# Router weights in four column groups, two transposes moved, and the first modulation vectors folded by VectorE

## The reference, cut to what matters

```python
# inside first_block
h = rms_norm(x, norm_mix); z = h @ w_in                      # 2048 columns: pool 512, q, k, v 512 each
y_attn = neighbourhood_attention(q, k, v, q_norm, k_norm, rpb) # 8 heads, a bias from rpb for each pair
x = x + concat(y_pool, y_attn) @ w_out
aff = softmax(rms_norm(x, norm_ffn) @ w_router)              # w_router is 1024 x 16
gates, idx = top_k(aff.T, 64)                                # per expert; then 16 gated experts
x = x + experts(...)
e = rms_norm(p @ w_ple_proj, norm_ple_post)                  # p is 512 x 256
# second_block, first layer
shift, scale, gate = split(silu(c) @ a_ada_w_2 + a_ada_b_2, 3)   # 1024 x 3072: three vectors of 1024
```

## Time and profile before

| what | value |
|---|---|
| median of 3 runs | 2246.3 us (2242.13 to 2247.63) |
| the profiled execution | 2247.05 us, its span 2245.3 us |
| PE busy | 2067.2 us (92%) |
| DVE busy | 906.8 us (40%) |
| ACT busy | 566.2 us (25%) |
| POOL busy | 147.7 us (7%), all of it in the first tenth of the span |
| mean granted clock of TensorE | 0.95 |

### The profile page before, as it was taken

One profiled execution on the slowest core, in us unless ns is written; L12 is line 12 of the kernel. 1 busy time (PEld: TensorE's weight loads), 2 busy tenths in 40 slices (PEclk: granted clock), 3 DMA queues, 4 the chain that ended last, 5 costly groups with the idle time before them and its releaser, 6 DMA issues.

```text
span 2245.3 us, 24651 instructions
## 1 busy us (share of the span) xinstructions
PE 2067.2 (92%) x9349; PEld 1243.1 (55%) x9349; DVE 906.8 (40%) x1457; ACT 566.2 (25%) x973; POOL 147.7 (7%) x86
## 2 busy tenths in 40 slices
PE   6989979999999999999999789999999998989798
PEld 5756763332222222222222277888887786867687
DVE  4754451111111111111111255465455727696963
ACT  4333241111101100011110244432233323553510
POOL 6568000000000000000000000000000000000000
PEclk9965879999999999999999899999999998999899
DMA  8831249999999999999999834553342212011010
GB/s 280 145 114 60 101 169 378 422 422 422 422 422 422 422 423 422 422 422 422 422 422 422 327 113 150 181 180 134 107 159 75 75 40 90 21 57 57 20 38 38
DMA packets 134346, 529.81 MB, mean 236 GB/s; under 512 B 10374, under 2 KB 58308, under 8 KB 85124
## 3 DMA queue, kind: packets, MB, share of 16 engines
q1 hardware_dynamic: 131988, 523.69, 59.4%
q0 software_dynamic: 1712, 3.06, 1.2%
q10 hardware_dynamic: 576, 2.10, 0.4%
HBM read 526.56 MB, written 2.23 MB: 236 GB/s over the span
## 4 chain that ended last, share of the span: by engine, by line
PE 56%; DMA 32%; DVE 7%; SPq 2%; ACT 2%; issue 2%; ACTq 0%; DVEq 0%
DMA w_expert<-in_w_up 15%; DMA w_expert<-in_w_gate 15%; PE bank L784 6%; PE bank L785 6%; PE bank L786 6%; PE bank L972 6%; PE bank L804 5%; PE bank L806 5%; PE bank L805 5%; PE bank L864 2%; SPq L617 2%; PE bank L878 1%; PE bank L816 1%; PE bank L982 1%; DMA raw<-in_w_ple_gate 1%
## 5 line engine op out<-in xcount | busy, mean ns | idle before, releaser
L972 PE MATMUL bank<-w_expert,chosen 128*64 128x512 f32 x2048 | 483.4, 602 | 61.9 <-DMA w_expert<-in_w_up 45.7
L972 PEld LDWEIGHTS bank<-w_expert,chosen 128*64 128x64 f32 x2048 | 130.5, 136 | 395.0 <-issue 233.2
L784 PE MATMUL bank<-act_hi,w_hi 128*128 128x512 f32 x656 | 269.8, 411 | 4.0 <-DVE act_lo L1489 2.0
L1443 DVE TENSOR_TENSOR w_lo<-raw,w_hi 128x2048 fp32r<-128x2048 f32 x75 | 181.9, 2426 | 204.5 <-ACT w_hi L1174 204.5
L786 PE MATMUL bank<-act_hi,w_lo 128*128 128x512 f32 x656 | 256.0, 390 | 0.0
L785 PE MATMUL bank<-act_lo,w_hi 128*128 128x512 f32 x656 | 255.9, 390 | 0.0
L1676 DVE TENSOR_TENSOR x_res<-x_res,bank 128x512 f32<-128x512 f32 x136 | 87.3, 684 | 412.0 <-PE bank L991 412.0
L982 PE MATMUL bank<-w_expert,hidden_t 128*64 128x512 f32 x1024 | 229.9, 596 | 5.8 <-ACT hidden_t L1318 4.6
L1174 ACT CAST w_hi<-raw 128x2048 fp32r<-128x2048 f32 x75 | 142.7, 1902 | 178.1 <-PE bank L806 173.7
L1698 DVE TENSOR_TENSOR hidden_rows<-gate_silu,bank 128x512 f32<-128x512 f32 x32 | 20.5, 683 | 363.7 <-PE bank L972 363.7
L1505 DVE RECIPROCAL full<-full 128x512 f32<-128x512 f32 x38 | 127.3, 3350 | 67.9 <-ACT full L1222 67.9
(11 more groups left out here) (235 smaller groups left out, 2549.7 us busy)
## 6 DMA issues: line engine op xcount, KB each, us to landing
w_expert<-in_w_gate SPq DMA_DIRECT2D x128, 1024.0 KB, 24.9
w_expert<-in_w_up SPq DMA_DIRECT2D x128, 1024.0 KB, 26.2
w_expert<-in_w_down SPq DMA_DIRECT2D x128, 1024.0 KB, 26.2
raw<-in_a_w_in SPq DMA_DIRECT2D x24, 1024.0 KB, 6.1
raw<-in_b_w_in SPq DMA_DIRECT2D x16, 1024.0 KB, 5.3
raw<-in_a_ada_w SPq DMA_DIRECT2D x12, 1024.0 KB, 8.1
raw<-in_b_ada_w SPq DMA_DIRECT2D x12, 1024.0 KB, 6.1
raw<-in_w_in SPq DMA_DIRECT2D x8, 1024.0 KB, 6.7
```

What stands on the lines that cost most here:

```text
L784: mm(b[:, :], hi[:, cols], ah[:, kc, :], start=(kc == 0), stop=False)
L972: last = mm(PS[b0 + n][HALF[x], :], XE[:, k % 4, HALF[k // 4]], WE[place][:, r], start=(k == 0), stop=(k == KD - 1), skip_group_check=True)
L1443: tt(WLO[w % 2][:, :], RAW[slot(n_of["W"][w])][:, :], WHI[w % 2][:, :].bitcast(F32), ALU.subtract).then_inc(lo_ready, 1)
```

## The change

The modulation vectors 0 to 2 are folded by DVE as the later ones are: A slabs 0 to 3 by `split_upto` between the slabs of `w_in`, A slabs 4 to 11 one each at attention items 2, 5, ..., 23. `ada_block` is gone from POOL, so the bias DMAs follow directly on the write-out of `rpb`. The router weights lie padded to 32 columns as stationary operand, one of four groups of 32 columns of the array for chunks kc and kc + 4, with 512 moving columns; ACT copies to four buffers; the four partial sums are added and turned by a second product with a folded identity. The transposes of p and their split stand between the halves of `W_OUT`, with p loaded first of its group. The two memsets stand before the router's result.

```diff
-        FOLD0 = 3
         def fold_done(i):
-            return 2 * (i - 4 * FOLD0 + 1)
+            return 2 * (i + 1)
...
# SP
+            sp.dma_start(PTOK[:, :, :], a["p"][0, 0].rearrange("(t p) d -> p t d", p=P)).then_inc(s_p, 16)
             sp.dma_start(GROW[:, :], bc(a["norm_ffn"], 0, D)).then_inc(s_grow, 16)
             sp.dma_start(CL[:, :], c_late).then_inc(s_late, 16)
-            sp.dma_start(WR[:, :, :], a["w_router"][0].rearrange("(k p) e -> p k e", p=P)).then_inc(s_wr, 16)
-            sp.dma_start(PTOK[:, :, :], a["p"][0, 0].rearrange("(t p) d -> p t d", p=P)).then_inc(s_p, 16)
+            sp.wait_ge(s_wz, 1)
+            sp.dma_start(WR[:, :, 0:NE], a["w_router"][0].rearrange("(k p) e -> p k e", p=P)).then_inc(s_wr, 16)
...
# POOL
-            pool.wait_ge(s_csil, 1)
-            ada_block(0, ACC1)
-
             for c in range(16):
                 pool.dma_start(BIAS[c * ROWS:(c + 1) * ROWS, :, :],
...
-            ada_block(1, ACC1)
-            ada_block(2, ACC1)
...
# PE, behind tm_unit(W_OUT[h], ...)
+                if h == 0:
+                    pe.wait_ge(s_p, 16)
+                    for c in range(2):
+                        b = begin(("pt", c))
+                        for t in range(NT):
+                            last = nc.tensor.transpose(b[:, t * P:(t + 1) * P], PTOK[:, t, c * P:(c + 1) * P], ident)
+                        last.then_inc(filled, 1)
...
             for kc in range(KD):
                 pe.wait_ge(freed["act"], fills[("norm", 1, kc)][2])
-                for t in range(NT):
-                    last = mm(lg[:, t * NE:(t + 1) * NE], FULL[kc % 2][:, t * P:(t + 1) * P], WR[:, kc, :],
-                              start=(kc == 0 and t == 0), stop=(kc == KD - 1), skip_group_check=True)
...
+                part = slice(kc % 4 * 32, (kc % 4 + 1) * 32)
+                last = mm(lg[part, :], WR[:, kc, :], XT4[kc % 4], start=(kc < 4), stop=(kc >= 4), skip_group_check=True)
+                if kc < 4:
+                    last.then_inc(r_used, 1)
+            last.then_inc(filled, 1)
+            pe.wait_ge(freed["act"], fills[("logits",)][2])
+            b = begin(("logits_t",))
+            for t in range(NT):
+                last = mm(b[:, t * NE:(t + 1) * NE], LGT[:, t * P:(t + 1) * P], FOLD[:, :], start=True, stop=True)
+            last.then_inc(filled, 1)
...
# ACT
-                if kc >= 2:
-                    act.wait_ge(r_used, kc - 1)
-                nc.scalar.copy(FULL[kc % 2][:, :], b[:, :]).then_inc(freed["act"], 1)
-            act.wait_ge(freed["dve"], fills[("logits",)][2])
+                if kc == 0:
+                    act.wait_ge(f_lo, f[0])
+                if kc >= 4:
+                    act.wait_ge(r_used, kc - 3)
+                nc.scalar.copy(XT4[kc % 4], b[:, :]).then_inc(freed["act"], 1)
+            nc.scalar.copy(LGT, take(("logits",))[:, :]).then_inc(freed["act"], 1)
+            act.wait_ge(freed["dve"], fills[("logits_t",)][2])
...
# DVE: fold() also for the first twelve slabs, and in the attention
+                    if j % 3 == 2 and len(folded) < 12:
+                        fold(len(folded))
                     tt(S1[j % 2][:, 0:n].rearrange("p (j k) -> p j k", k=ROWS),
...
+            nc.vector.memset(WR[:, :, :], 0.0).then_inc(s_wz, 1)
+            nc.vector.tensor_reduce(FOLD[:, :], ident.rearrange("p (j e) -> p e j", j=4)[:, 0:NE, :], AX.X, ALU.add
+                                    ).then_inc(s_wz, 1)
...
+                if h == 0:
+                    for c in range(2):
+                        split_lo(("pt", c), PH[:, c, :], PL[:, c, :])
+            split_upto(W_PROJ)
             nc.vector.memset(POS[:, :, :], 0.0).then_inc(k_step, 1)
+            for x in (Y[:, :], SELT[:, :]):
+                nc.vector.memset(x, 0.0).then_inc(zeroed, 1)
```

More of the change, by code:

```diff
@@ L150, in bass_kernel @@
         RANK = at("topk_rank", 190, [NE, S])
-        WR = at("w_router_sb", 192, [P, KD, NE])
+        WR = at("w_router_sb", 194.5, [P, KD, P // 4])
+        FOLD = at("router_fold", 195.5, [P, NE])
         AFF = at("affinity", 192.5, [P, NT, NE + 1])
@@ L313, in note_norm @@
             if k == 1:
-                note(("logits",), "dve")
+                note(("logits",), "act")
+                note(("logits_t",), "dve")
         def note_attn(tag, n):
@@ L348, in bass_kernel @@
                 note(("wout", h, t), "dve")
+            if h == 0:
+                for c in range(2):
+                    note(("pt", c), "lo")
         note_norm(1)
         note(("aff_t",), "dve")
-        for c in range(2):
-            note(("pt", c), "lo")
         for h in range(2):
@@ L441, in bass_kernel @@
         freed = {"act": sem("bank_read_by_act"), "dve": sem("bank_read_by_dve"), "lo": f_lo}
-        ada_step, ada_fold = sem("ada_step"), sem("ada_folded")
+        ada_fold = sem("ada_folded")
         s_const, s_rows, s_x = sem("consts_loaded"), sem("rows_loaded"), sem("x_loaded")
@@ L515, in tile_of @@
             return ap.rearrange("p (i r) -> p r i", r=NT)[:, t, :]
+        XT4, LGT = [FULL[0][:, :], FULL[1][:, :], SQ[0][:, :], SQ[1][:, :]], FULL[0][:, :]
         def from_grid(ap):
@@ L622, in _ @@
                     _, kind, i = stream[N_E - 4 + g]
-                    sp.wait_ge(lo_ready, i + 1) if kind == "W" else sp.wait_ge(ada_step, ada_done(i))
+                    sp.wait_ge(lo_ready, i + 1) if kind == "W" else sp.wait_ge(ada_fold, fold_done(i))
                 if g == 3:
@@ L818, in ada_ready @@
             def ada_ready(b_):
[L819 to L822, removed]
+                pe.wait_ge(ada_fold, fold_done(4 * b_ + 3))
             def ada_cols(b_, acc):
@@ L914, in _ @@
             last.then_inc(filled, 1)
[L915 to L920, removed]
             pe.wait_ge(f_lo, 18)
@@ L1271, in _ @@
                 split_hi(("ot1", c), BH[:, 4 + c, :].rearrange("p (r c) -> p c r", r=ROWS), in_ap=from_grid)
-            for h in range(2):
-                split_upto(W_OUT[h][1] + 1)
+            split_upto(W_OUT[0][1] + 1)
+            for c in range(2):
+                split_hi(("pt", c), PH[:, c, :])
+            split_upto(W_OUT[1][1] + 1)
             stats(1, lambda t: (freed["dve"], fills[("wout", 1, t)][2]))
@@ L1416, in _ @@
             tt, ts, stt = nc.vector.tensor_tensor, nc.vector.tensor_scalar, nc.vector.scalar_tensor_tensor
-            folded = list(range(4 * FOLD0))
+            folded = []
             def fold(i):
@@ L1423, in fold @@
                 part = raw3(n, 2)
-                if i % 4 == 0 and b_ > FOLD0:
+                acc = ACC1 if b_ < 3 else ACC2
+                if i == 0:
+                    dve.wait_ge(s_csil, 1)
+                if i % 4 == 0 and b_ not in (0, 3):
                     dve.wait_ge(filled, fill_no(("ada", b_ - 1)))
@@ L1429, in fold @@
                     if i % 4 == 0 and k == 0:
-                        ts(ACC2[:, :], part[:, k, :], c, None, ALU.mult).then_inc(ada_fold, 1)
+                        ts(acc[:, :], part[:, k, :], c, None, ALU.mult).then_inc(ada_fold, 1)
                     else:
                         dve.wait_ge(ada_fold, fold_done(i) - 2 + k)
-                        stt(out=ACC2[:, :], in0=part[:, k, :], scalar=c, in1=ACC2[:, :], op0=ALU.mult, op1=ALU.add
+                        stt(out=acc[:, :], in0=part[:, k, :], scalar=c, in1=acc[:, :], op0=ALU.mult, op1=ALU.add
                             ).then_inc(ada_fold, 1)
@@ L1622, in _ @@
                         norm_behind(1, t)
+                if h == 0:
+                    for c in range(2):
+                        split_lo(("pt", c), PH[:, c, :], PL[:, c, :])
+            split_upto(W_PROJ)
             nc.vector.memset(POS[:, :, :], 0.0).then_inc(k_step, 1)
-            b = take(("logits",))
-            dve.wait_ge(r_used, KD)
+            for x in (Y[:, :], SELT[:, :]):
+                nc.vector.memset(x, 0.0).then_inc(zeroed, 1)
+            b = take(("logits_t",))
             lg = b[:, 0:NT * NE].rearrange("p (t e) -> p t e", e=NE)
@@ L1663, in select_inputs @@
                 last.then_inc(d_sel, 1)
-            for x in (Y[:, :], SELT[:, :]):
-                nc.vector.memset(x, 0.0).then_inc(zeroed, 1)
             nc.vector.tensor_copy(POSN, POS[:, :, 0]).then_inc(d_cur, 1)
```

15 lines of the change are left out of this document (1 added, 14 removed).

## The result

The changed kernel takes 2251.99 us (median of 9 executions, 2250.84 to 2254.82) against 2246.3 (9 executions, 2242.13 to 2247.68): ratio 1.0033, 95% interval 1.0024 to 1.0042. By the medians that is 5.7 us more (0.25%), inside the 6.7 us (0.3%) that the prediction called no change; the ratio's 0.33% lies just outside it, so the result is at the upper edge of "no change". The profiled execution took 2254.82, the slowest of the nine, with a span of 2252.8, where the one before had a span of 2245.3.

A forecast was written before the change was run, and what follows sets the result against it. PE bounds the w_in product, attention (half clock) and router, transfers the experts; early bias DMAs meet saturated transfers. 15 - 3.3 + 0.5 - 1.1 - 4.9 - 1.0 = +5.2 on the median 2246.3 gives 2251 us, range 2235 to 2259.

The forecast's parts named there:

- slabs late: In the w_in product, early bias DMAs delay slabs; PE idles 13.2 us, plus 1.8 at half clock: +15.
- attention's start: Last w_lo before the attention, no longer beside POOL's modulation work, takes 2.28 instead of 5.75 us: -3.3.
- folds in the attention: Eight DVE folds of about 2.6 us among the attention items, mostly caught up in waits for scores: +0.5, bounds 0 and 8.
- p: Between output halves: top-k starts 2.3 us earlier, the 8 transposes add 1.2 to the chain: -1.1.
- router: Router product in four overlapping column groups at half clock takes 8.6 us instead of 13.48: -4.9; -7 at full clock.
- memsets: Two memsets of 0.48 us each leave the chain: -1.0.
- The hold-up: In w_in, 25 to 26 us of bias transfers land the fourth slab at 64.7, needed by 51.5; third's wait inside.
- Rival B: In w_in, bias stays within the fourth slab's 12.8 us margin: no +15, so -9.8 and 2236.5; chance 0.28.
- D: Rival: transfers mix worse than the sum of their work, stall 20, time 2257; chance 0.11.
- C: Rival: router column groups don't overlap, +3.1 instead of -4.9, with the stall 2259.5; chance 0.12.
- E: Rival: TensorE's clock doesn't fall before the attention, which runs partly at 2.4 GHz: some -30, 2221; chance 0.05.

The follow-up runs named there:

- e6: e1 with p turned and split behind aff_t again and the memsets before the first gather, as in the kernel before: 2239.95 us, ratio 0.9982.
- e8: The changed kernel with 8 of the 16 bias DMAs issued early and 8 held until the fifth w_in slab is split: 2241.18 us, ratio 0.9985.
- e3: The kernel before with only the router, p and memset edits; modulation folds and bias DMAs in their old places: 2236.11 us, ratio 0.9965.
- e7: e1 with each fold in the attention cut in two, one instruction at one item and the other at the next: 2235.67 us, ratio 0.9964.
- e5: e1 with all eight chunks of the router product written to one column group and accumulated there: 2240.47 us, ratio 0.9983.
- e11: e7 with both the bias DMAs held only until the fourth w_in slab is split and proj behind the first top-k maximum: 2234.92 us, ratio 0.9960.
- e9: e7 with proj on PE started only behind the first maximum of the top-k: 2233.99 us, ratio 0.9955.
- e10: e7 with the bias DMAs held only until the fourth slab of w_in is split: 2235.21 us, ratio 0.9956.
- e1: The changed kernel with POOL's 16 bias DMAs held until the fifth slab of w_in is split: 2238.46 us, ratio 0.9974.

## Why the prediction was right, by its own steps

It said 2251, and 2252 came. The time is right, and so is what makes it: the early bias DMAs hold up a slab of w_in, PE waits for it, and the router takes back part. One step inside this, which slab PE waits for, is wrong. That the sum is right to about 1 us is in part luck, since errors cancel. Against the profiled execution before, up to the experts' first matmul:

| term | predicted | measured | from |
|---|---|---|---|
| slabs late | +15 | +16.9 | last w_lo before the attention starts at 138.34, before at 121.45 |
| attention's start | -3.3 | -3.2 | scores +13.7 |
| folds in the attention | +0.5 | +1.5 | 103.7 us between first and last scores, before 102.3 |
| p | -1.1 | -1.2 | e6's rows |
| router | -4.9 | -7.7 | last turned norm to exponential 6.5 us, before 14.2 |
| memsets | -1.0 | -1.0 | ranks to gather 1.81, before 2.82 |
| gather's clock | none | -1.3 | 3.65 us, before 4.97 |
| sum | +5.2 | +4.0 | experts' start +4.1 |

Two stretches without an edit are not in the table, and each is within the scatter of the marks: from the last matmul of the output product to the last turned norm 8.2 us, before 7.5 (PE at a granted 0.50 from 306.4 to 309.8), and from the last scores to the output product 12.6, before 12.9. The profiled executions go on to differ by 5.0 at the last combine and 7.5 at the end; the medians differ by 5.7. So the table bears out the terms to about 1 us each, not the total to the tenth.

- **The hold-up.** The transfer work was well sized: 25 to 26 us were forecast and the third slab landed 26.6 later. The step that failed is which slab PE waits for. The prediction computed the fourth (needed at 51.5, landing at 64.7) and wrote that the third's wait "is inside this one, not added". It is the other way round: the third makes PE wait 14.68 us. The fourth landed at 68.1 (64.7 forecast; it was issued 5.9 us later than before), its w_lo was done at 72.35, and PE's first matmul with it starts at 72.73, against 55.84 before: PE has no further wait, because it was itself 17 us late by then, but with 0.4 us to spare. That the size came out near is luck: the two margins happen to be alike, 12.8 us for the fourth and 11.8 for the third. Behind the wait PE runs at a granted 0.50 until 64.1 us, 5.3 us at half rate, which is about 2.6 us of work; less the 0.6 us by which w_in's first matmul started earlier, that is nearly all of the other 2.2 us (1.8 forecast).
- **Rival B**, that the margin of 12.8 us covers it: out, by the same rows. e8 shows what was right in it: half of the DMAs would nearly have been free. **D**, stall 20: the wait is 14.7 and the whole term 16.9, out.
- **The attention's start.** w_lo took 2.56 us instead of 5.75, and PE waits 3.13 for the first exponential instead of 6.38. e3, which has the old `ada_block`, has a w_lo of 5.02 there.
- **Folds.** The forecast took 2.6 us for each and put POOL's part at 1 or 2 us in the sentences on the exclusion that the Trainium skill states (SBUF — State Buffer, "SBUF: two separate sides"). The measured 1.5 and the rows of 3.5 to 4.4 us beside POOL's windows speak for that reading, though e7 didn't isolate it.
- **Router.** The term most mis-sized, by 2.8 us, mainly because I costed it at half clock, with -7 named for full clock: it ran at a granted 1.00. No run takes apart the 0.7 us beyond -7. The overlap of all four groups, which no row had shown, holds in the first round (e5). **C**, no overlap, is out by e5. **E**, the clock staying up in the attention, is out: 0.50 again.
- **Behind the experts.** From the last combine to the end the changed kernel's profiled execution lost another 2.5 us, where nothing is edited and the forecast counted nothing. The clock makes half of that. 70.5 us behind the last combine, at the start of the same product of a later layer, the changed kernel's row is the first and that of the kernel before the second:

```profile
1364.50:1368.00 3.50, 3.50 (x10) 2.72 (x9) 3.40 (x7) 2.65 (x4) 0.00 (x0) 0.51 0.74 279
1359.50:1363.00 3.50, 3.50 (x15) 2.57 (x15) 3.40 (x7) 2.60 (x4) 0.00 (x0) 1.00 0.76 284
```

Ten matmuls against fifteen: from there on everything is 1.3 us later, and smaller steps make the rest. Over the thirteen kernels the last part takes 956.0 to 957.0 us in seven, the one before among them, and 958.2 to 958.8 in six. All six have this stretch at half clock, and of the seven only e3 has it, which gains 1.2 us later. No edit goes with it: e11 has it, and e9 and e10, whose edits it joins, have not. The rest of the 2.5 us stays open.

## What to carry to other kernels

When an engine is freed, list the DMAs behind its old work: they move with it. Sixteen small transfers, issued from 50 us on, cost nothing, and issued from 19 us on they cost 17 us, in the same kernel. Give late loads a wait on a progress mark, and don't leave it to an engine's slowness to hold them back. For a stream of slabs compute the margin of each one in flight, also of those issued ahead of the intruder. And when a large rewrite measures as no change, time its halves apart: here one was worth -8 us (e3), and the other, once its DMAs were held back and its folds cut in two, cost nothing (e7 at 0.9964 against e3 at 0.9965).

## What the hardware showed beyond that

- Being issued first did not protect a load. The third slab was issued 4.2 us ahead of the first bias DMA and still landed 26.6 us later than before. The Trainium skill (DMA: Bandwidth & Descriptors, "Queues, rings and completion order") says that a DMA engine takes turns between the queues that have work, a packet at a time; 87 GB/s at a share of 1.18, where the slabs alone run at 394 and 1.05, fits that, and so do the counts. From 36 to 46 us of the changed kernel the queue of POOL's DMAs and that of SP's moved almost the same number of packets (then MB and share of 16 engines):

```profile
q0 software_dynamic: 319, 0.50, 66.7%
q1 hardware_dynamic: 326, 0.34, 48.1%
```

By these rows a packet of the first took about 0.33 us of one engine's time (an estimate: 66.7% of 16 engines' 10 us over 319). Where the slabs ran alone, from 26 to 38 us in e1, 2097 packets took 104.2% of 16 engines' 12 us, 0.10 us each. So a slab that gets every second turn, behind packets some three times as long, lands much later than the bias's bytes alone would suggest. In the old place, 79 to 102 us of the kernel before, it was the same, 658 packets against 668, but there PE was busy in all 23 us. The counts are not as even in every stretch, 698 against 897 from 22 to 44 us, so turn by turn is what they suggest, not what they prove.
- The issuing instructions are held up too. Four reloads of x occupied SP's queue for 16.67 us, against 6.76 us in the kernel before, and single slab issues took 7.70 and 14.08 us instead of 0.4, while the bias DMAs were in transfer. So SP's later loads, the fourth slab among them (issued at 36.77, before at 30.9), also start late.
- Four column groups did a round of fp32 matmuls with 32 columns of weights and 512 moving columns in 1.07 us against 3.63 us in one group, 3.4 times as fast, with all four begun within 0.02 us.
